# Moving the context tokens' dense layer of a diffusion block into the first expert pass, with row slots in pairs

## The reference, cut to what matters

```python
# each layer, for the latents and (in layer 0) for the context
h = rms_norm(x) * (1 + scale) + shift            # modulation from c or c_ctx
p = h @ w_in                                     # q, k, v of mixers A, B, C and three gates
ya, yb, yc = attention A, B, C                   # latents read latents and context, context reads context
m = sigmoid(ga) * (ya @ wa) + sigmoid(gb) * (yb @ wb) + sigmoid(gc) * (yc @ wc)
x = x + gate1 * (m @ w_out)
# expert retrieval, per token: 8 heads x 16 picks
q = h2 @ wq;  s = q . keys;  top-16 of each side, top-16 of the 256 sums -> e, g = softmax
act = gelu(u[e] . h2);  x = x + gate2 * sum((g * act) * v[e])
```

## Time and profile before

| | us |
|---|---|
| median of 3 runs (3233.8 to 3236.12) | 3234.09 |
| the profiled execution's own time | 3236.32 |
| its span in the trace | 3234.5 |
| TensorE busy | 2762.8 (85%) |
| VectorE busy | 1882.7 (58%) |
| ScalarE busy | 1272.2 (39%) |
| GpSimd busy | 850.2 (26%) |
| mean granted TensorE clock | 0.957 |

### The profile page before, as it was taken

How to read it: one execution, slowest core, us unless ns; L and a number is a source line. 1 busy time by engine, 2 the same in 40 slices (tenths; PEclk the granted TensorE clock), 3 DMA queues, 4 the chain that set the end, 5 groups by cost and what they waited for, 6 DMA issues and landing times.

```text
span 3234.5 us, 31361 instructions
## 1 busy us (share of the span) xinstructions
PE 2762.8 (85%) x10516; PEld 1585.7 (49%) x10516; DVE 1882.7 (58%) x4371; ACT 1272.2 (39%) x3305; POOL 850.2 (26%) x790
## 2 busy tenths in 40 slices
PE   6899989989778997878889999888898977878786
PEld 2686668867234553223334454337798822222222
DVE  0335973337656559886545445454955688755444
ACT  1323752224424433444433333334643444443333
POOL 0000000002323334543444444430000144443332
PEclk7899989989978999999999999998999899999999
DMA  8321002227999999999999999993135499999996
GB/s 330 121 90 66 21 27 95 101 78 305 421 414 421 421 421 385 422 421 421 422 421 418 420 418 421 422 385 114 31 120 179 156 421 421 421 421 421 422 421 286
DMA packets 135665, 981.85 MB, mean 304 GB/s; under 512 B 15184, under 2 KB 15312, under 8 KB 16720
## 3 DMA queue, kind: packets, MB, share of 16 engines
q0 software_dynamic: 112032, 810.08, 60.6%
q1 hardware_dynamic: 23184, 167.09, 13.7%
q10 hardware_dynamic: 288, 2.69, 0.2%
HBM read 978.74 MB, written 1.05 MB: 303 GB/s over the span
## 4 chain that ended last, share of the span: by engine, by line
PE 50%; DMA 28%; DVE 13%; ACT 6%; issue 2%; POOL 0%; SPq 0%; ACTq 0%; DVEq 0%; POOLq 0%
DMA att<-experts_in,att 25%; PE ps L992 20%; PE ps L549 6%; PE ps L551 6%; PE ps L550 6%; DVE att L1933 4%; DMA ring<-stream_in 3%; ACT att L1338 3%; PE ps L938 2%; PE ps L673 1%; PE ps L813 1%; DVE ring_lo L1510 1%; DVE stat L1696 1%; PE ps L581 1%; PE ps L593 1%
## 5 line engine op out<-in xcount | busy, mean ns | idle before, releaser
L992 PE MATMUL ps<-att 128*128 128x512 f32 x3072 | 1490.8, 621 | 312.5 <-ACT att L1338 309.9
L1933 DVE CUSTOM_DVE_ANT_0 att<-att 128x1024 f32<-128x1024 f32 x768 | 938.3, 1224 | 767.1 <-DMA att<-experts_in,att 759.1
L1463 POOL DMA_INDIRECT att<-experts_in,att x768 | 839.8, 1093 | 1863.7 <-PE ps L992 1138.2
L992 PEld LDWEIGHTS ps<-att 128*128 128x128 f32 x3072 | 555.2, 193 | 1203.2 <-ACT att L1338 702.0
L1331 ACT ACTIVATE att<-att 128x1 f32<-128x1 f32 x768 | 155.1, 202 | 1049.2 <-DVE att L1933 1045.7
L1510 DVE TENSOR_TENSOR ring_lo<-ring,wt_hi 128x2048 fp32r<-128x2048 f32 x84 | 192.4, 2291 | 283.0 <-ACT wt_hi L1078 283.0
L1338 ACT ACTIVATE att<-const,att 128x128 f32<-128x128 f32 x768 | 308.2, 401 | 75.7 <-PE ps L992 4.2
L1333 ACT ACTIVATE att<-att 128x1 f32<-128x1 f32 x768 | 226.1, 294 | 24.9
L1078 ACT ACTIVATE wt_hi<-ring 128x2048 fp32r<-128x2048 f32 x84 | 160.3, 1910 | 148.1 <-PE ps L551 148.1
L549 PE MATMUL ps<-h,wt_hi 128*128 128x256 f32 (+1 forms) x448 | 155.4, 347 | 15.1 <-DVE h L1525 13.9
L550 PE MATMUL ps<-h,wt_hi 128*128 128x256 f32 (+1 forms) x448 | 150.5, 336 | 0.0
(11 more groups left out here) (188 smaller groups left out, 3318.4 us busy)
## 6 DMA issues: line engine op xcount, KB each, us to landing
ring<-stream_in SPq DMA_DIRECT2D x155, 1024.0 KB, 5.9
att<-experts_in,att POOLq DMA_INDIRECT x768
att<-bias_in POOLq DMA_DIRECT2D x16, 256.0 KB, 2.9
x<-x_in ACTq DMA_DIRECT2D x1, 2048.0 KB, 7.8
att<-stream_in SPq DMA_DIRECT2D x2, 1024.0 KB, 7.0
spare<-stream_in SPq DMA_DIRECT2D x1, 1024.0 KB, 22.0
out<-att SPq DMA_DIRECT2D x1, 1024.0 KB, 3.9
const<-const_in ACTq DMA_DIRECT2D x1, 576.0 KB, 4.0
```

The lines of the kernel that those rows point to most:

```text
L992: last = mm(ps[:, d, :], diag[:, m % DIAGS, :], rows[:, m % SLOTS, D + 512 * d:D + 512 * (d + 1)], start=(n % HK == 0), stop=(n % HK == HK ...
L1463: nc.gpsimd.indirect_dma_start(out=rows[:, m % SLOTS, :], out_offset=None, in_=experts_in, in_offset=bass.IndirectOffsetOnAxis(ap=index[:, ...
L1933: v.tensor_tensor_reduce(out=u_row, in0=u_row, in1=h_tok[:, n // HK, :], scale=1.0, scalar=0.0, op0=ALU.mult, op1=ALU.add, accum_out=dots[ ...
```

## The change

- The front's attention, `head_norm`, `merge` and `w_out` are for the 256 latents. `proj_both` makes the q units with 256 tokens and the k and v units with 512 as before. The normalised input stays in place, and `again=True` goes.
- In pass 0 the context's norm, 12 query units, 24 attention steps, head norm, 48 merge items, 8 output units, second norm and `wq_plain` are ticks, with fp32 products on raw pairs. SyncE loads for it 6, 18 and 4 more pairs (queries, merge, output); each of these weights is read a second time.
- The modulation of layer 1 moves to pass 1, as do seven of the eight quarters of the context's picks.
- There are two tick tables for a pass (`PICKS_AT`, `TOKENS_AT`), and ticks are called after every second pick (`due`).
- A slot now holds two picks for each of 64 tokens. `copy_tokens` makes four copies for one, indices and gates are written in four parts, the diagonal matrices are 128x64, and TensorE takes two slots at a time: 8 MATMULs of 64 columns of the array, alternating between its halves. `row_used` counts pairs of slots.

```diff
-STREAMS = [[0, 1], [0]]
+STREAMS = [[0], [0]]
-TICKS = [spread(1, (18, 30), (2 * MOD_TICKS + NORM_TICKS, 56), (WQ_TICKS, 46), (UPDATE_TICKS + TOK_TICKS, 8),
-                (KEY_TICKS + QUARTERS * PICK_TICKS, 108)),
-         spread(1, (TOK_TICKS + UPDATE_TICKS, 8), (NORM_TICKS + proj_ticks(1), 230), (UPDATE_TICKS, 8)),
...
+PICKS_AT = [spread(1, (PICK_TICKS, 14), (6 * SIDE_TICKS, 20), (PICK_TICKS, 16), (PICK_TICKS, 30), (4 * PICK_TICKS, 128)),
...
+TOKENS_AT = [spread(22, (NORM_TICKS, 10), (CTX_Q_TICKS, 24), (ATTENTION_TICKS, 60), (HEAD_TICKS, 8), (MERGE_TICKS, 58),
+                    (WOUT_TICKS, 14), (NORM_TICKS, 10), (WQ_TICKS, 26), (UPDATE_TICKS + TOK_TICKS, 8), (FIRST_TICKS, 14)),
+             spread(1, (TOK_TICKS + UPDATE_TICKS, 10), (2 * MOD_TICKS, 90))
...
+def due(at, n):
+
+    return at.count(n - 1) + at.count(n) if n % 2 else 0
...
+    QKV_AT.append(run(RUN_PAIRS[CTX_Q], "raw", again=first))
+    MERGE_AT.append(run(MERGE_PAIRS, "raw", again=merge))
+    WOUT_AT.append(run(WOUT_PAIRS, "raw", again=merge + MERGE_PAIRS))
...
# TensorE, proj_both
+                    n = N_LAT if k < FIRST_KEY else T
...
# TensorE, the context's merge (one item is one tick)
+                    if item >= 6:
+                        pe.wait_ge(prod_done, 3 * DC + (item - 6) // 2 + 1)
+                    count = DC if item % 2 == 0 else 4
...
+                        last = mm(ps[:, 2 + item % 6, 0:N_CTX], raw_slot(p0, b), src, start=(c == 0), stop=(c == count - 1))
+                    last.then_inc(merge_done, 1)
+                    yield
...
# TensorE, gather
-                    pe.wait_ge(diag_ready, m + 1)
+                    pe.wait_ge(diag_ready, m + 2)
                     for d in range(2):
-                        last = mm(ps[:, d, :], diag[:, m % DIAGS, :], rows[:, m % SLOTS, D + 512 * d:D + 512 * (d + 1)],
-                                  start=(n % HK == 0), stop=(n % HK == HK - 1))
+                        for s in range(2):
+                            last = mm(ps[HALF * s:HALF * (s + 1), d, :], diag[:, (m + s) % DIAGS, :],
+                                      rows[:, (m + s) % SLOTS, D + 512 * d:D + 512 * (d + 1)],
+                                      start=(n % HK == 0), stop=(n % HK == HK - 2))
                     last.then_inc(row_used, 1)
...
# ScalarE, the context's attention (tick k) and merge (tick item)
+                    if 0 <= k - 3 < steps:
+                        copy_probt(k - 3)
+                    if 0 <= k - 1 < steps:
+                        exps(k - 1)
+                    yield
...
+                    if item % 2 == 1:
+                        g = item // 2
+                        act.wait_ge(merge_done, 6 * DC + item)
...
+                        nc.scalar.activation(sig_c[:, g % 4, :], ps[:, 2 + (item - 1) % 6, 0:N_CTX], ACT.Sigmoid)\
+                            .then_inc(sig_ready, 1)
+                    yield
...
# ScalarE, copy_tokens and the diagonal matrix
+                for s in range(2):
+                    for j in range(2):
+                        last = nc.scalar.activation(dup[HALF * j:HALF * (j + 1), tt, s, half * 512:(half + 1) * 512],
+                                                    ps[HALF * s:HALF * (s + 1), tok_bank(r, part), :], ACT.Copy)
...
-                    nc.scalar.activation(diag[:, m % DIAGS, :], ident, ACT.Copy, scale=acts[:, n:n + 1])\
+                    nc.scalar.activation(diag[:, m % DIAGS, :], fold, ACT.Copy, scale=acts[:, n:n + 1])\
...
# VectorE, the context's merge (tick item)
+                    if item % 2 == 0 and item:
+                        g = item // 2 - 1
...
+                        dve.wait_ge(sig_ready, 3 * DC + g + 1)
+                        dve.wait_ge(merge_done, 6 * DC + item)
...
# GpSimd
-                        pool.wait_ge(row_used, m - SLOTS + 1)
+                        pool.wait_ge(row_used, (m - SLOTS) // 2 + 1)
```

More of the change, by code:

```diff
@@ L113, in idle, with ran_out @@
         yield
-def together(first, second):
-    for _ in first:
-        next(second)
-        yield
-    for _ in second:
+CTX_SIDES = [(0, 2), (0, 3)] + [(1, g) for g in range(4)]
+def ran_out(work):
+    for _ in work:
         assert False
@@ new lines, in context_head_norm @@
+            def context_head_norm():
+                yield
+                for h in range(4):
+                    pe.wait_ge(cn_sq, 4 + h + 1)
+                    for t in range(2):
+                        last = mm(ps[:, 4, h * TT + t:h * TT + t + 1], head_sq_c[:, h, tile_of(t)], ones[:, 0:1],
+                                  start=True, stop=True)
+                last.then_inc(cn_sum, 1)
+                yield
+                yield
+                for h in range(4):
+                    pe.wait_ge(head_diag_ready, 4 + h + 1)
+                    mm(ps[:, 4 + h, 0:N_CTX], ones, head_diag_c[:, h, :, :].rearrange("p t k -> p (t k)"),
+                       start=True, stop=True).then_inc(head_spread, 1)
+                yield
+                yield
+                yield
@@ L983, in update, with gather @@
                 yield from idle(UPDATE_TICKS - 2)
-            def gather(r, front):
-                for n in range(PICKS):
+            def gather(r, picks, tokens):
+                for n in range(0, PICKS, 2):
                     m = r * PICKS + n
@@ L994, in gather @@
                     last.then_inc(row_used, 1)
-                    for _ in range(TICKS[r].count(n)):
-                        next(front)
-                for _ in front:
-                    assert False
-            def context_front():
-                yield from idle(18)
+                    for _ in range(due(PICKS_AT[r], n + 1)):
+                        next(picks)
+                    for _ in range(due(TOKENS_AT[r], n + 1)):
+                        next(tokens)
+                ran_out(picks)
@@ L1346, in gather @@
                                 .then_inc(acc_copied, 1)
-                    for _ in range(TICKS[r].count(n)):
-                        next(front)
-                for _ in front:
-                    assert False
+                    for _ in range(due(PICKS_AT[r], n)):
+                        next(picks)
+                    for _ in range(due(TOKENS_AT[r], n)):
+                        next(tokens)
+                ran_out(picks)
+                ran_out(tokens)
             def rest_of_picks(r):
```

773 lines of the change are left out of this document (517 added, 256 removed).

## The result

The changed kernel takes 3186.6 us, the median of four executions: 3184.22, 3185.14, 3188.05 and one of 3391.88, which ran at a mean granted clock of 0.689 (the others at 0.851 to 0.856) and stays out of the comparison, which leaves a median of 3185.14. Before, in the same job, it was 3233.95 us (3232.66 to 3236.12). The ratio is 0.985, 95% interval 0.9831 to 0.987: 1.5% faster. The forecast was 3182 us. The profiled execution has 3184.22 us and a span of 3182.4.

What follows compares the result with a forecast made beforehand. TensorE's products bound the front, DMA bytes the first two passes. From 3236.3: -176 -28 +70 +4 = 3106, then +25 +30 +20 -5 +8 = 3184 profiled, 3182 us median; range 3145 to 3215.

Steps and rivals of the forecast that it cites:

- Front, -176 -28 = -204: Before pass 0: latents-only layer 0 attention saves 176 us, the 12 query units with shorter products 28.
- Bytes, +70: In the passes: 28 more weight pairs, 29.4 MB at 421 GB/s, cost 70 us, as the DMA engines are full.
- Merge, +30: Pass 0, context merge: TensorE, ScalarE and VectorE waits make 219 us of batches against 189 of bytes, loss 30.
- Attention, +25: Pass 0, context attention: ScalarE with table loads needs 6.4 us a batch against 4.98 of DMA, loss 25 us.
- The Trainium skill's switch of 2.66 us: ScalarE's table switches: the skill adds a 1.38 us drain behind the load, making an attention batch 2.8 us longer.
- Smaller stretches, +20; VectorE, -5: Pass 0's output units, head norm and two norms lose 20 us; spreading the context's picks over pass 1 returns 5.
- Clock, +8: TensorE's granted clock, halved at times in the attention stretch, costs 8 us in all (0 to 150).
- Bytes alone: Rival for the passes: eight slots bridge long batches, stalls of 78 us shrink under 20, total 3112 us; chance 0.20.
- The clock falls: Rival for pass 0, chiefly merge: TensorE at 1.2 GHz, 3253 us at two fifths, 3372 throughout; chance 0.15.
- Halves do not overlap: Rival: the array's halves do not overlap with 512 columns, 1.72 us more a pair on TensorE's path, 3266; chance 0.03.
- Tables cost twice: Rival: a 1.28 us drain at each of 96 table switches in attention and merge, 3284 us; chance 0.02.
- the three signs of being wrong: In the merge: DMA rate holding 421 GB/s, or granted clock under 0.8; or pairs of picks taking 3.4 us.

Runs made afterwards that it cites:

- one table less: The changed kernel with the Sigmoid of the context's merge in pass 0 replaced by a Copy: 3163.7 us, ratio 0.9779.
- 43 us of bytes less: One block of 16 loaded of each of the merge's 18 weight pairs: in the changed kernel 3174.04 us, with ScalarE's and VectorE's merge work two ticks later 3141.48.
- Square: The changed kernel with Exp replaced by Square in the context's attention in pass 0: 3171.74 us, ratio 0.98.
- the steps in twos: The changed kernel with two context attention steps behind every second pair of slots in place of one behind every pair: 3200.09 us, ratio 0.9892.
- the later elementwise work: The changed kernel with ScalarE and VectorE starting the context merge's work two ticks later, same computation: 3151.78 us, ratio 0.9743.

## Why the prediction was right, point by point

- **Front, -176 -28 = -204.** Measured -194.7. The latents' part is right (242.7 us; 243 was said). The query units gave 24.4, not 28, and from the last update of x to the first gather it takes 55.6 us in place of 49.7, 6 more; `copy_tokens`, which the sum had at 4 for both passes, lies in that piece. So the first gather is at 564, not near 552.
- **Bytes, +70.** Measured 71, as the windows show.
- **Merge, +30.** Measured 34 by the rate. The stage of 219 us on record took 223.2: twelve (even, odd) batches of 9.2 to 9.3 us (9.2 was said) and a first one of 10.6, seven (odd, even) of 7.7 to 8.2 (7.7), single ones of 4.9 to 6.4 (5.2). Its rate is 356 GB/s (364 was said). That the ring of waits is the cause is shown three ways: cutting it gives 35 us, one table less gives 23, and 43 us of bytes less leave the stage's length alone. Mis-sized was only what the tables cost: the expectation counted the load in the (even, odd) batches alone, 15 us, and these gave 16.5; the other 6 of the 23 came from the first batch and from those of a single odd item.
- **Attention, +25.** Measured 15. This is the term that was mis-sized. The mechanism holds (ScalarE busy 94%, Square gives 15 us back), but a batch is 5.97 us, not 6.4: I took 2.08 us for two picks and 1.2 for two Exps with their reads, and the rows have 1.74 (854.97 to 856.71) and, with the reads beside the next Exp, 1.0. The 30 pairs took 169.0 us, not 184, at 376 GB/s from 754 to 895 us (365 was said). The working also had the merge's first four weight pairs loaded beside the attention; they are issued ahead of it.
- **The Trainium skill's switch of 2.66 us** ("ScalarE: Activation LUTs", section "What ACT_TABLE_LOAD costs") was left out of the sum. The trace does not agree with it here: load at 853.67, Gelu at 854.97, 1.30 us. By 2.66 a batch would be 8.7 us, as an estimate.
- **Smaller stretches, +20; VectorE, -5.** The net of 15 is about right: the loss outside merge and attention went from 20 to 36 us. The places are right in part. Head norm (24.6 us for four pairs, 5 over their bytes; 4 was said), the output's two double batches (9.46 each) and the experts' queries (84.0; 83) came as worked out. What was missing is the searches of the other heads (sides) beside the first norm, 9 us of lost rate at 655 to 700 us where nothing had been counted for them; and the stretch that VectorE bounded did not go, it is at 1345 to 1375 us now, where VectorE is busy 29.2 of 30 us.
- **Clock, +8.** No row here shows a cost. Merge ran at 1.00; the attention at 0.89, with ScalarE's batches back to back; pass 2 at 0.73 (0.99 before) with the DMA at 411 GB/s as before. The fear had a ground, as the steps in twos show.
- **Sum.** Passes: 148 was said, 136.6 measured. Layer 1 and the rest came out 6 us longer (2124.9 to 2506.5 is 381.6 us, 377.9 before, with ScalarE busy 193.0 us there for 185.3, 7.7 more, where 7 had been said for `copy_tokens`; the last pass 675.9, 673.6 before). -194.7 + 136.6 + 3.7 + 2.3 = -52.1, where the terms on record gave -52.3. The front, with its share of `copy_tokens`, gave 5 us less than said, the merge cost 4 more and the end 6 more; the attention cost 10 less and the clock 8 less. These misses cancelled to within a microsecond. The total owes that to luck, its large terms do not.
- **Rivals.** *Bytes alone*: the slots do not bridge the batches, 65 us of stalls were added. *The clock falls*: refuted for the merge, its place, by the 1.00 there. *Halves do not overlap*: refuted by 1.94 us, and its price of 3266 was too low; forced, it is 3308. *Tables cost twice*: refuted by the 5.97 us from load to load, in which no drain has room. None of the three signs of being wrong showed: the merge ran at 356 GB/s and a granted clock of 1.00, the pairs took 1.9 us.

## What to carry to other kernels

When small pieces of one computation are interleaved with another, an engine's busy sum says little. Write down the ring of waits between the engines through one batch and ask which value is needed in the batch that makes it: moving the consumer two steps later cost nothing and gave 35 us, all that the merge had lost, and batching steps to save table loads made a new ring, with TensorE near half its clock behind a wait, and cost 13. Compare stages over the same work, not over the same stretch of time. Before removing bytes or work from a stage, look at whether its length follows them.

Work that was moved beside a stage whose DMA engines are full was paid there in bytes, whatever the other engines have to spare: 195 us less of front cost 137 us of passes here, 71 of them bytes. The kernel that beat both, the change with the later elementwise work, stands at 3151.78 us, 2.6% under before.

## What the hardware showed that I had not expected

- Products of 64 columns in the two halves of the array, issued in turn, take 1.94 us for eight MATMULs of 512 columns at 2.4 GHz, against 3.65 for the same eight in one half. The change as built hangs on it: without it, 3308 us.
- In pass 2 the mean granted clock fell from 0.99 to 0.73, a mix of 2.4 and 1.2 GHz, with TensorE busy for 60% (392 of 654 us, 522 of 655 before), and 654 us at 411 GB/s stayed as they were. With the products in one half, pass 2 had TensorE busy for 486 of 655 us, a clock of 0.98 and the same 410 GB/s; the kernel's mean clock was 0.949 and its time 121 us longer. A clock under 1 cost nothing where the transfers set the pace. In the attention's steps in twos, where TensorE stood on the path, the 0.54 of a batch came with sixteen products in 6.65 us.
- A stage can have TensorE at 178.26 of 179 us busy and still move 409 GB/s beside it.
